# Reordering the opening loads of a two-layer encoder, keeping its normalized memory in SBUF, and cutting the last stages into halves

## The reference

```
for i in range(2):
    u = rmsnorm(h, norm_mix_g[i]);  proj = u @ w_in[i]            # 1024 x 7168
    y_conv = conformer_conv(proj[..., :2048], ...)                # gated, 31-tap depthwise conv, layernorm, silu
    y_attn = diff_attention(q, k, v, positions, lam, ...) @ w_attn_out[i]
    h = h + (gates[:D] * y_conv + gates[D:] * y_attn) @ w_out[i]
    m = rmsnorm(mem, norm_mem_g[i])                               # mem: 256 x 1024, the same in both layers
    h = h + cross_attention(rmsnorm(h, norm_x_g[i]), m, w_xq[i], w_xkv[i], w_xo[i])
    h = h + hier_moe(rmsnorm(h, norm_ffn_g[i]), ..., w1[i], w3[i], w2[i])   # 32 experts, 2 per token
return rmsnorm(h, final_norm_g)
```

## Time and profile before

| | |
|---|---|
| median of 3 runs | 1791.09 us (1790.96 to 1793.93) |
| profiled execution: own time, span | 1792.14 us, 1790.3 us |
| busy in the span | PE 84%, PEld 57%, DVE 35%, ACT 29%, POOL 3% |
| moved by DMA | 532.94 MB, mean 298 GB/s |

### The profile page before, as it was taken

The page is one execution under the profiler, slowest core; times in us unless marked ns, Lnnn a source line. Parts: engine busy times, 40 slices in busy tenths (PEclk is TensorE's granted clock), DMA queues, the critical chain, the costliest instruction groups (busy, mean ns, idle before and its releaser), DMA issues.

```text
span 1790.3 us, 24014 instructions
## 1 busy us (share of the span) xinstructions
PE 1501.6 (84%) x9680; PEld 1013.8 (57%) x9680; DVE 618.4 (35%) x1012; ACT 524.7 (29%) x819; POOL 58.0 (3%) x102
## 2 busy tenths in 40 slices
PE   5999999999877676767699999999987767676765
PEld 5778889897323232323277978998843323232322
DVE  4657786654000010101054668775520101010101
ACT  4535555553110100000153465635431000000001
POOL 3011000000000000000000200000000000000000
PEclk9999999999998888898999999999989989888988
DMA  8535335754899999999955452357469999999995
GB/s 267 196 118 183 123 141 178 259 223 188 340 425 423 425 423 425 423 425 424 421 192 176 124 193 103 142 193 277 182 262 396 424 425 424 424 424 424 425 423 246
DMA packets 108943, 532.94 MB, mean 298 GB/s; under 512 B 7784, under 2 KB 7976, under 8 KB 67654
## 3 DMA queue, kind: packets, MB, share of 16 engines
q1 hardware_dynamic: 105440, 524.12, 73.4%
q0 software_dynamic: 3424, 7.83, 1.8%
q10 hardware_dynamic: 12, 0.05, 0.0%
HBM read 525.68 MB, written 2.10 MB: 295 GB/s over the span
## 4 chain that ended last, share of the span: by engine, by line
PE 56%; DMA 37%; DVE 3%; ACT 2%; issue 1%; SPq 1%; PEldq 0%; DVEq 0%; ACTq 0%
DMA ring<-in_w_dram 36%; PE ps L1993 10%; PE ps L1612 7%; PE ps L1617 6%; PE ps L1613 6%; PE ps L1646 5%; PE ps L1647 5%; PE ps L1652 5%; PE ps L1962 2%; PE ps L1694 2%; DMA ring<-in_w_xkv_dram 1%; PE ps L1751 1%; PE ps L2003 1%; PE ps L1774 1%; PE ps L1946 1%
## 5 line engine op out<-in xcount | busy, mean ns | idle before, releaser
L1099 DVE TENSOR_TENSOR weight_split<-ring,weight_split 128x1024 fp32r<-128x1024 f32 x224 | 270.5, 1222 | 166.6 <-ACT weight_split L717 163.9
L717 ACT ACTIVATE weight_split<-ring 128x1024 fp32r<-128x1024 f32 x224 | 234.0, 1058 | 227.6 <-PE ps L1652 89.3
L1962 PE MATMUL ps<-ring,big 128*32 128x512 f32 x2048 | 238.7, 608 | 63.3 <-DMA ring<-in_w_dram 35.9
L1993 PE MATMUL ps<-ring,big 128*32 128x512 f32 x1024 | 181.0, 872 | 119.7 <-DMA ring<-in_w_dram 114.9
L1612 PE MATMUL ps<-operand_split,weight_split 128*128 128x256 f32 x896 | 228.3, 292 | 4.8 <-ACT weight_split L717 3.2
L1613 PE MATMUL ps<-operand_split,weight_split 128*128 128x256 f32 x896 | 220.0, 283 | 0.0
L1962 PEld LDWEIGHTS ps<-ring,big 128*32 128x32 f32 x2048 | 74.0, 111 | 206.5 <-issue 206.4
L1612 PEld LDWEIGHTS ps<-operand_split,weight_split 128*128 128x128 f32 x896 | 171.6, 192 | 18.2 <-issue 13.1
L1993 PEld LDWEIGHTS ps<-ring,big 128*32 128x32 f32 x1024 | 46.0, 152 | 231.9 <-issue 226.1
L1613 PEld LDWEIGHTS ps<-operand_split,weight_split 128*128 128x128 f32 x896 | 171.9, 192 | 2.3 <-issue 2.2
L985 ACT ACTIVATE big<-ps,cst 128x256 f32<-128x256 f32 x32 | 15.1, 473 | 524.8 <-PE ps L1951 524.8
(11 more groups left out here) (243 smaller groups left out, 1506.4 us busy)
## 6 DMA issues: line engine op xcount, KB each, us to landing
ring<-in_w_dram SPq DMA_DIRECT2D x248, 1024.0 KB, 17.6
ring<-in_w_dram SPq DMA_DIRECT2D x64, 2048.0 KB, 19.3
ring<-in_w_in_dram SPq DMA_DIRECT2D x28, 2048.0 KB, 8.4
ring<-in_w_xkv_dram SPq DMA_DIRECT2D x8, 2048.0 KB, 7.9
ring<-in_w_attn_out_dram SPq DMA_DIRECT2D x4, 2048.0 KB, 7.7
ring<-in_w_conv_out_dram SPq DMA_DIRECT2D x4, 2048.0 KB, 8.0
ring<-in_w_out_dram SPq DMA_DIRECT2D x4, 2048.0 KB, 7.8
big<-in_w_dram SPq DMA_DIRECT2D x8, 1024.0 KB, 12.9
```

Of the source, the lines that this page charges most:

```text
L717: act.activation(split_quarter(k, 0), landed_quarter(k), ACT.Copy).then_inc(w_hi, 1)
L1099: dve.tensor_tensor(split_quarter(k, 1), landed_quarter(k), split_quarter(k, 0).bitcast(F32), ALU.subtract).then_inc(w_lo, 1)
L1962: last = pe.matmul(ps[CAP * j:CAP * (j + 1), 1, :], xe[:, k, e * CAP:(e + 1) * CAP], pair_slot(j)[:, k, :], start=(k == 0), stop=(k == DC ...
L1993: last = pe.matmul(ps[CAP * j:CAP * (j + 1), 3, :], up_t[:, f, e, :], w[:, f, half * SLAB:(half + 1) * SLAB], start=(f == 0), stop=(f == F ...
```

## The change

Seven edits are made together. (1) SP issues the identity ahead of the memory rows, and the remaining constants behind slab `a0` instead of ahead of it. (2) POOL issues no small DMA until slab `xk0` has landed; positions, lambdas and router parameters wait for slab `a0` too. (3) The turned memory is kept in `memT` without a gain (`keep_mem`, a plain copy), and each layer's gain goes into the split itself: eight instructions of 128 x 256 on ACT and on DVE in place of four of 128 x 512. Layer 1's extra scaling, the store to HBM and the load back are gone. (4) The lambda dots and exponentials are moved from behind the rope angles to behind the first two gated products, the rest of them behind the conv products. (5) PE multiplies the identity twelve times before the parameter rows are there. (6) A down slab is fetched in two transfers of 1 MB, first halves of both experts first, and PE waits for the second halves only half way through the down products. (7) At the end each 128-row half has its own chain, with the root table loaded ahead, and the rows are scaled and stored in column halves.

```diff
         def _(sp):
+            sp.dma_start(cst[:, 0:P], consts[:, 0:P]).then_inc(ident_in, 16)
             sp.dma_start(memN, mem[0].rearrange("(s p) d -> p s d", p=P)).then_inc(mem_in, 16)
-            sp.dma_start(cst[:, 0:P], consts[:, 0:P]).then_inc(ident_in, 16)
...
-                for e in range(2):
-                    left(False, 2 + e)
-                    sp.dma_start(down_slot(4 + e),
-                                 w2[L, 2 * i + e].rearrange("(p c) n -> p c n", p=P)).then_inc(down_in[e], 16)
+                for k in range(2):
+                    for e in range(2):
+                        if k == 0:
+                            left(False, 2 + e)
+                        sp.dma_start(down_slot(4 + e)[:, 2 * k:2 * k + 2, :],
+                                     w2[L, 2 * i + e].rearrange("(p c) n -> p c n", p=P)[:, 2 * k:2 * k + 2, :]
+                                     ).then_inc(down_in[k][e], 16)
...
+                if L == 0:
+
+                    pool.wait_ge(slab_in[0], 16)
...
                 if L == 0:
+
+                    pool.wait_ge(slab_in[1], 16)
+                    attention_params()
                     router_params()
-                    pool.wait_ge(st_mg2, 4)
-                    pool.dma_start(mem_t_dram[0], big[:, 2, :]).then_inc(st_msto, 16)
...
+            act.activation(spare, cst[:, C_ID:C_ID + 1], ACT.Sqrt)
             for s in range(TT):
+                act.wait_ge(added[s], act.snap(u))
                 act.activation(uT[:, s * FC:(s + 1) * FC, :].rearrange("p c t -> p (c t)"), h_sum(s), ACT.Square,
                                accum_out=ss[:, s:s + 1]).then_inc(fin_ss, 1)
-            act.wait_ge(fin_var, 1)
-            act.activation(ss, ss, ACT.Sqrt).then_inc(fin_sq, 1)
+                act.wait_ge(fin_var, s + 1)
+                act.activation(ss[:, s:s + 1], ss[:, s:s + 1], ACT.Sqrt).then_inc(fin_sq, 1)
...
-            def mem_gain(i, j, done):
-
-                gain = pk[:, i, 0:K_WR].rearrange("p (c r) -> p c r", c=DC)[:, 2 * j:2 * j + 2, R_MEM]
-                dst = memT if i == 0 else chunks(1 + i)
+            dve.sem_inc(st_pk, 1)
+
+            def keep_mem(j):
+
                 dve.wait_ge(st_mt, j + 1)
-                dve.tensor_tensor(dst[:, 2 * j:2 * j + 2, :], ps[:, 2 + j, :].rearrange("p (c t) -> p c t", c=2),
-                                  gain.unsqueeze(2).to_broadcast([P, 2, T]), ALU.mult).then_inc(done, 1)
+                dve.tensor_copy(memT[:, 2 * j:2 * j + 2, :],
+                                ps[:, 2 + j, :].rearrange("p (c t) -> p c t", c=2)).then_inc(st_mg, 1)
...
+                for c in range(DC):
+                    if L == 0 and c in (2, 4):
+                        keep_mem(c // 2 + 1)
+                    dve.wait_ge(*due(mem_hi, c + 1))
+                    dve.scalar_tensor_tensor(mem_s[1][:, c, :], memT[:, c, :], mem_gain(L, c),
+                                             mem_s[0][:, c, :].bitcast(F32), ALU.mult, ALU.subtract).then_inc(mem_lo, 1)
...
             pe.wait_ge(ident_in, 16)
+            for _ in range(12):
+                pe.matmul(ps[:, 0, 0:P], ident, ident, start=True, stop=True)
...
-                    for e in range(2):
-                        pe.wait_ge(down_in[e], n * 16 + 16)
                     for f in range(FC):
+                        if f % 2 == 0:
+                            for e in range(2):
+                                pe.wait_ge(down_in[f // 2][e], n * 16 + 16)
```

More of the change, by code:

```diff
@@ L408, in encoder @@
         ahead_in = [[sem(f"ahead_slab_{j}_half_{k}_landed") for j in range(2)] for k in range(2)]
[L409 removed]
+        down_in = [[sem(f"down_slab_{e}_half_{k}_landed") for e in range(2)] for k in range(2)]
         slab_in = [sem(f"dense_slab_landed_{i}") for i in range(LAND)]
@@ L1182, in _ @@
                     rope_angles()
-                    lambdas()
                 def gated(j):
@@ L1235, in _ @@
                 products(1)
+                if L == 0:
+                    lambdas()
                 dve.wait_ge(router_in, 16 * 5 * LAYERS)
@@ L1663, in turn_norm @@
                         turn_rows(begin(job), src, j).then_inc(full[bank(job)], 1)
-                col_jobs("xk.", "xk0", (0, 1), mem_s, have=(mem_lo, 0, 2))
+                col_jobs("xk.", "xk0", (0, 1), mem_s, have=(mem_lo, 0, 1))
                 settle()
```

116 lines of the change are left out of this document (57 added, 59 removed).

## The result

| | before | after |
|---|---|---|
| median of 4 runs each, side by side | 1792.24 us | 1781.24 us (1779.08 to 1784.98) |
| ratio, 95% interval | | 0.9943 [0.9930, 0.9955] |
| profiled execution: own time, span | 1792.14, 1790.3 us | 1784.98, 1783.2 us |

It is faster, by some 10 to 11 us where 15.2 were forecast.

The account below looks back on a forecast made before the run. PE was taken to bound the dense stages and DMA the expert stages. Terms -9.0 + 0.5 - 3.2 - 3.5 = -15.2 us gave 1775.9 us; its own range was 1773 to 1779, with rivals 1770 to 1781.5.

Parts of the forecast that it names:

- The opening: Kernel start to layer 0's norm turn: identity first and POOL held back give 9.0 us less, range 6.5 to 10.8.
- The step from the low product to the turn: Layer 0, first low-part product to norm's turn: 1.3 us less, as the four extra products are gone.
- The further 1.8 us for memory products at full clock: Opening, upper bound: if identity products keep the array at full clock, memory products shrink and 1.8 us more is gained.
- The step into layer 1: Entry to layer 1: eight subtractions in place of four cost 0.5 us more, bounds 0 and 1.0.
- The end: After the last products: separate chains for row halves and a smaller last store give 3.5 us less, bounds 2.7 and 4.2.
- The halved downs: Expert stream: down slabs in two transfers cost nothing, ±0.15 us for each of 28 bound pairs, ±4.2 us.
- halved downs are dear: Rival, expert stream: halves cost 0.14 us for each of 28 pairs, 3.9 us, total 1779.8; chance 0.13.
- The last pair: Last expert pair: half its down products run before the last bytes land, 3.2 us less, bounds 1.7 and 3.4.
- Dense layer 0 "at nothing": Transfers and DVE work moved out of the opening cost nothing, covered by dense work that PE makes at full rate.
- Fixed price for each transfer: Rival, expert stream: two more transfers a pair make it slower than before, 1804 at 1 us each pair; chance 0.02.
- Late gain rows: Rival, opening: memory or ACT's gain rows land 3 us later than reckoned, total 1778.9; chance 0.13.
- swallowed opening: Rival, after the opening: a slab or the taps are late by as much as was gained, total 1784.9; chance 0.03.

Follow-up runs that it names:

- cut_by_partitions: Changed kernel with each down matrix in two transfers of 64 partitions with 16 KB rows, in place of 128 partitions with 8 KB; ratio 1.289 by the median.
- pool_at_once: Changed kernel without POOL's two waits on slabs, so that its small transfers issue from the start; 1782.84 us in one execution.
- end_only: Kernel before the change with only the split end added, down matrices whole; ratio 0.9981, 3.4 us less.
- opening_only: Changed kernel with whole down matrices and the old end, leaving the new opening and what moved out of it; ratio 0.9936, 11.5 us less.

## Why the prediction was wrong, and where it was right

Measured 11.7 us less over three timings; forecast 15.2. By its steps:

- **The opening, -9.0: right.** Over 15 profiles with the new opening (without `cut_by_partitions` and `pool_at_once`) the turn is at 31.0 on average (29.1 to 32.7; forecast 31), over three with the old one at 39.7. That is 8.7. The memory's landing, the start of its products at 10.44 (10.4) and the low product at 20.31 (20.9) came as worked out. The slab landed at 13.3, 1.4 us later than worked out, and was not missed. The step from the low product to the turn, which was to give 1.3 us, is 10.3 us in 12 of these profiles (forecast 10.1), and 11.8 in the changed kernel's first profile and two others, where the clock fell to half in it; there it gave nothing. The further 1.8 us for memory products at full clock came in two of the 15 (3.84 us, turns at 29.06 and 29.23). The cause was right as well, with one correction: POOL's standing still was counted for the memory too, and the memory lands as early without it (squares at 7.09 for 7.04); it is the slab that needs it.
- **The step into layer 1, +0.5: right** (-3.69 became -3.16). The eight subtractions took 3.28 us (3.4).
- **The end, -3.5: right**: -3.4 by `end_only`, 7.2 us from L2023's start for 7.1.
- **The halved downs: the step that failed.** The prediction read 9.93 against 9.79 us, 0.14 for each pair, then took off "0.3 of it perhaps PE's own" and put the stream at zero. There was nothing to take off: the period rose by 0.15, and by 0.15 again where only the rows were short. Over the two streams that is 4.0 us in the profile (2.1 and 1.9), the rival "halved downs are dear", whose price of 3.9 was met. What the price hangs on is the length of the rows, not the number or the size of the transfers; that the ups are slower per byte for their 8 KB rows too follows from this and was not tested on them.
- **The last pair, -3.2: met in its rows, not in the time.** -2.9 in the first profile, between 0.5 and 3 in others, by the clock of its products and by last ups that land up to 1.2 us late.
- These two together were forecast at -3.2 and gave 0 (0.9935 with halves, 0.9935 without; ±2.5 us). -9.0 + 0.5 - 3.5 = -12.0 is left, and 11.7 was measured. That the two agree so closely is in part luck: the next point speaks of 2 us more in dense layer 0, and the opening alone gained 11.5 us where 8.5 was forecast for it.
- **Dense layer 0 "at nothing": right for the moved work, wrong as a promise.** Each slab was there in time, `a0` with 2.5 us to spare where 5 were reckoned. But 1.7 or 3.4 us come and go with TensorE's clock. Twelve profiles with the new opening and no fill average 393.5 us from turn to sum, three with the old one 391.4; behind the pause in layer 0 a low stretch came in 11 of 13 profiles with the new opening and in none of the three with the old. So the opening seems to have a part in it; it is open how, since `pool_at_once`, with its turn at 40.42, has 393.3, and `opening_only` 390.0. The Trainium skill, in "TensorE: Matmul & The Clock Gate", Part 1, says that one and the same kernel has more or fewer of its matmuls at the low clock from run to run; the profiles of one kernel agree (dense layer 1 of the changed kernel: 393.74 and 391.30).
- **The rivals.** Fixed price for each transfer: none is seen, two and four transfers give the same 29.82. The Trainium skill has one of about 2 us in "DMA: Bandwidth & Descriptors", section "Anatomy of one DMA", which is on DMAs issued from GpSimd; in this stream of SP's no run shows it in the period. Late gain rows and a swallowed opening did not happen.

## What to carry to other kernels

In a stream that the DMA bounds, read the rate of each kind of transfer and believe a difference of a per cent: it is repeated in each round, and cutting a transfer is free only if its rows stay as long. A cut can gain at the last round, some 3 us in the rows here, so weigh it against the rounds that pay; cutting in the last round alone was no better here. Keep small DMAs of another queue back while the first large ones are needed. Work put into a TensorE pause of about 2 us kept the clock up here; if it pays at all, then with work no longer than the pause, and the gain in time is not shown. And where one step scatters by several us, as the entries here, check a term of 3 us by its rows and not by the total.

## What the runs showed of the hardware

- Transfers of 64 partitions with rows of 16 KB ran at 217 GB/s, with the engines' busy share at 1.02, beside 420 for 128 partitions.
- A row more costs some 9 ns on its engine at rows of 4 to 16 KB (periods 29.67, 29.82, 30.11), and the number of transfers, two or four, nothing in the period (29.82 both).
- Small POOL transfers took a 2 MB landing from 11.5 to 20.6 us.
- In the dense stages low stretches of TensorE's clock mostly cost 1.7 us or 3.4 each. Behind the pause in front of the v projection, of 1.7 to 3.0 us, one was there in 26 of 34 layers, and in none of the six layers in which the pause was filled. The pauses without one were 1.7 to 2.65 us long, so the length alone doesn't decide.
